# A hybrid decoder block on one core: the norm's weight in the gather's eviction, a tail in halves, and eight gate pieces inside masking and inversion

## The reference

```python
def hybrid_mixer(xn, mem_n, ...):
    p = xn @ w_in
    p_rwkv, p_swa, p_mem = jnp.split(p, [RWKV_PROJ, RWKV_PROJ + SWA_PROJ], axis=-1)
    y_rwkv = rwkv7_branch(p_rwkv, ...)      # 8 heads of 64, a recurrence over 256 tokens
    y_swa = swa_sink_alibi_branch(p_swa + b_swa, swa_sinks)
    y_mem = memory_cross_branch(p_mem, mem_n, w_mem_kv)
    branches = (y_rwkv, y_swa, y_mem)
    merged = jax.nn.sigmoid(xn @ w_gate[0]) * (branches[0] @ w_branch[0])
    for bi in range(1, N_BRANCH):
        merged = merged + jax.nn.sigmoid(xn @ w_gate[bi]) * (branches[bi] @ w_branch[bi])
    return merged @ w_out

def sparse_moe(xn, ...):                    # top 4 of 32 experts per token
    logits = (xt @ w_router + b_router)
    top_vals, top_idx = lax.top_k(logits, TOP_K)
    gates = jax.nn.softmax(top_vals, axis=-1)
    ...
        h = x_pad[tok] @ w1[e] + b1[e]      # 1024 x 2048
        return clamped_swiglu(h) @ w2[e] + b2[e]   # 1024 x 1024

h = h + hybrid_mixer(rms_norm(h, attn_norm_w), rms_norm(mem, mem_norm_w), ...)
h = h + sparse_moe(rms_norm(h, ffn_norm_w), ...)
return rms_norm(h, final_norm_w)
```

## Time and profile before

| | us |
|---|---|
| median of 3 runs | 1307.2 (1306.89 to 1308.43) |
| the profiled execution | 1308.61 |
| its span in the profile | 1306.8 |
| TensorE busy | 1222.7 (94%) |
| VectorE busy | 355.6 (27%) |
| ScalarE busy | 196.4 (15%) |

### The profile page before, as it was taken

The page is one execution under the profiler, slowest core; times in us unless marked ns, Lnnn a source line. Parts: engine busy times, 40 slices in busy tenths (PEclk is TensorE's granted clock), DMA queues, the critical chain, the costliest instruction groups (busy, mean ns, idle before and its releaser), DMA issues.

```text
span 1306.8 us, 15506 instructions
## 1 busy us (share of the span) xinstructions
PE 1222.7 (94%) x6554; PEld 597.6 (46%) x6554; DVE 355.6 (27%) x597; ACT 196.4 (15%) x377; POOL 0.2 (0%) x4
## 2 busy tenths in 40 slices
PE   8998989999999999999998989898988989898986
PEld 7886778888653333333333323232333323232322
DVE  2146472211234123221222212121222212121222
ACT  2224522200111011110101111010101111010102
POOL 0000000000000000000000000000000000000000
PEclk9999989999999999999999999999999999999999
DMA  9353201595379999999999999999999999999993
GB/s 356 106 165 129 65 4 34 191 383 200 142 268 429 427 428 429 427 428 427 428 430 427 430 427 428 429 428 430 427 427 431 427 429 428 427 431 426 429 426 164
DMA packets 51840, 449.74 MB, mean 344 GB/s; under 512 B 5552, under 2 KB 17968, under 8 KB 26704
## 3 DMA queue, kind: packets, MB, share of 16 engines
q1 hardware_dynamic: 51312, 447.49, 82.9%
q10 hardware_dynamic: 480, 1.57, 0.4%
HBM read 448.00 MB, written 1.05 MB: 344 GB/s over the span
## 4 chain that ended last, share of the span: by engine, by line
PE 63%; DMA 30%; DVE 4%; ACT 1%; issue 1%; SPq 0%; PEldq 0%; DVEq 0%
PE ps L461 62%; DMA ring<-in_w_exp 30%; DVE ring L1415 1%; PE ps L971 0%; DMA xrows<-in_x 0%; DVE upper L1506 0%; PE ps L704 0%; ACT ring L1171 0%; PE ps L613 0%; DVE ring L1412 0%; ACT ring L1197 0%; DVE upper L1463 0%; DVE merged L1441 0%; ACT upper L1140 0%; PE ps L982 0%
## 5 line engine op out<-in xcount | busy, mean ns | idle before, releaser
L461 PE MATMUL ps<-ring,upper 128*64 128x512 f32 (+4 forms) x2928 | 572.5, 535 | 38.9 <-DMA ring<-in_w_exp 35.2
L461 PEld LDWEIGHTS ps<-ring,upper 128*64 128x64 f32 (+2 forms) x2928 | 181.5, 138 | 390.4 <-issue 325.9
L461 PE MATMUL ps<-upper 128*64 128x512 f32 (+8 forms) x1644 | 288.6, 440 | 18.9 <-DMA upper<-in_w_exp 8.9
L461 PEld LDWEIGHTS ps<-upper 128*64 128x64 f32 (+4 forms) x1644 | 145.4, 161 | 154.5 <-issue 133.0
L461 PE MATMUL ps<-xT,ring 128*128 128x256 f32 x672 | 149.9, 381 | 0.4 <-DVE xT L1380 0.4
L461 PEld LDWEIGHTS ps<-xT,ring 128*128 128x128 f32 x672 | 126.5, 190 | 18.9 <-issue 1.8
L1688 DVE TENSOR_TENSOR upper<-ps,merged 128x512 f32<-128x512 f32 x32 | 22.1, 692 | 374.6 <-PEq L942 374.6
L1709 DVE TENSOR_TENSOR xrows<-xrows,ps 128x1024 f32<-128x1024 f32 x32 | 39.1, 1221 | 299.8 <-PE ps L461 299.8
L1289 ACT ACTIVATE upper<-upper 128x512 f32<-128x512 f32 x32 | 20.2, 631 | 555.5 <-DVE upper L1691 555.5
L1295 ACT ACTIVATE factors<-ps 64x512 f32<-64x512 f32 x63 | 37.3, 592 | 206.0 <-PEq L964 205.2
L461 PE MATMUL ps<-factors,upper 128*128 128x512 f32 x128 | 63.1, 617 | 0.0
(11 more groups left out here) (214 smaller groups left out, 478.2 us busy)
## 6 DMA issues: line engine op xcount, KB each, us to landing
ring<-in_w_exp SPq DMA_DIRECT2D x140, 2048.0 KB, 32.7
upper<-in_w_exp SPq DMA_DIRECT2D x48, 2048.0 KB, 33.6
ring<-in_w_gate SPq DMA_DIRECT2D x9, 1024.0 KB, 5.1
ring<-in_w_exp SPq DMA_DIRECT2D x8, 1024.0 KB, 22.0
ring<-in_w_in SPq DMA_DIRECT2D x8, 896.0 KB, 11.7
ring<-in_w_in SPq DMA_DIRECT2D x8, 640.0 KB, 3.9
ring<-in_w_branch SPq DMA_DIRECT2D x5, 1024.0 KB, 5.2
ring<-in_w_mem_kv SPq DMA_DIRECT2D x4, 1024.0 KB, 4.9
```

The costliest lines, as they stand in the source:

```text
L461: return pe.matmul(o, l, r, start=start, stop=stop, skip_group_check=True)
```

## The change

In words:

- `fill_points` gets eight new points: after the own values and transposes of the masking stage (`("gram", 0)` to `("gram", 3)`) and in levels 1 to 4 of the inversion. Each holds one piece: the four gate pieces of unit 0, then those of unit 1. The branch pieces of these units come in the first chunk's points. "rest" keeps 23 pieces. To free banks 6 and 7, the fourth `gram` group goes into banks 0 and 1 once the first is masked (`GRAM_BANK`), and `own_values` use banks 2 and 3.
- ScalarE loads the sigmoid's table ahead of the masking stage, and does the new gates between its copies.
- The norm's weight is no longer loaded as rows. `hn` is the rows times the root alone, done by ScalarE in two halves. The weight comes in as a column per partition ("ffnp", permuted on the host as the rows of `hn` are) when VectorE evicts the gather (`gathered` moves from ScalarE to VectorE).
- The transposes of the gates move into the first expert's up product, behind its fourth step. Two dummy matmuls are added in routing.
- Expert 30's second matrix is loaded as one load of 2 MB and two of 1 MB; its down product has the transposes for expert 31 and for the gates after its third quarter. The last down product uses bank 4 and `act_last`, and its four dummies are gone.
- The last scatter, addition, square, scaling and store are done by halves of 512 columns.

The diff, cut to its core:

```diff
+GRAM_BANK = (0, 2, 4, 0)
 def fill_points():
-    points = [(ch, s) for ch in range(NCH) for s in "abc"] + ["norm0", "norm1", "rest"]
-    counts = [1] * (3 * NCH) + [2, 3]
+    points = [("gram", i) for i in range(4)] + [("level", j) for j in range(1, LEVELS - 1)]
+    points += [(ch, s) for ch in range(NCH) for s in "abc"] + ["norm0", "norm1", "rest"]
+    counts = [1] * (len(points) - 3) + [2, 3]
     counts.append(PIECES * N_FILL - sum(counts))
+    sequence = [0, 1, 2, 3, 6, 7, 8, 9, 4, 5, 10, 11] + list(range(12, PIECES * N_FILL))
...
@@ SyncE
-                    load_w2(q, a, r, very_first and r == 0)
+                    if very_first and r == 0:
+                        load_w2(q, a, r, 0)
+                    elif count < GROUP and r == count - 1:
+                        load_w2(q, a, r, 2)
+                    else:
+                        load_w2(q, a, r)
...
-                    sp.wait_ge(final_sb, q * TT + t + 1)
-                    sp.dma_start(out[0, t * P:(t + 1) * P, :], outrow[:, t, :]).then_inc(stored, 16)
+                    for b in range(2):
+                        half = slice(b * 512, (b + 1) * 512)
+                        sp.wait_ge(final_sb, q * (2 * TT) + 2 * t + b + 1)
+                        sp.dma_start(out[0, t * P:(t + 1) * P, half], outrow[:, t, half]).then_inc(stored, 16)
@@ TensorE
+                if n == 3:
+                    pe.wait_ge(gram_sb, 1)
...
             pe.wait_ge(gram_sb, 2)
-            own_values(0, 0)
+            own_values(0, 2)
+            fill(("gram", 0))
+            fill(("gram", 1))
             pe.wait_ge(gram_sb, 3)
             pe.wait_ge(inv0_sb, 1)
             turn_inverse(0)
+            fill(("gram", 2))
             pe.wait_ge(gram_sb, 4)
-            own_values(1, 6)
+            pe.wait_ge(av_sb, 2)
+            own_values(1, 2)
+            fill(("gram", 3))
             pe.wait_ge(inv0_sb, 2)
             turn_inverse(1)
...
                     if j > 1:
                         turn_inverse(t)
+                if j < LEVELS - 1:
+                    fill(("level", j))
...
             gather_half(0, 1)
+            keep_awake(1, 7, const("iota"))
             pe.wait_ge(chosen_sb, 2)
...
+            keep_awake(1, 7, const("iota", 0, P))
             gather_half(1, 0)
             gather_half(1, 1)
-            pe.wait_ge(gates_sb, 1)
-            for t in range(TT):
-                last = pe.transpose(ps[0:NE, 3, t * P:(t + 1) * P], gates[:, t, :], ident)
-            last.then_inc(gT_ps, 1)
+            def turn_all_gates(c):
+                if c == 3:
+                    (the same wait and transposes)
...
-                    if final and i < 3:
-                        keep_awake(1, 4, hn[:, 0, 0:512])
+                    if between:
+                        between(i)
                 pe.wait_ge(slots_used, n + (NMIX + 1))
                 pe.sem_inc(down_ps, 1)
-                if final:
-                    keep_awake(1, 4, hn[:, 0, 0:512])
...
-            up(g, r, E, N, 0, None, first)
+            up(g, r, E, N, 0, turn_all_gates if very_first else None, first)
...
+                def turns(i):
+                    if i == 2:
+                        turn(E + 1)
+                        turn_gates(N, False)
+                if last:
+                    down(q, g, r, E, 2, False, turns)
@@ ScalarE
+            act.activation(ss[:, 7:8], epsc[:, 0:1], ACT.Sigmoid)
-            act.dma_start(ffnw, ffn_norm_w.to_broadcast([P, D])).then_inc(late_loaded, 16)
...
+                act.wait_ge(norm_scale, t + 1)
+                for b in range(2):
+                    half = slice(b * 512, (b + 1) * 512)
+                    act.activation(hn[:, t, half].rearrange("p (c q) -> p q c", c=4), xrows[:, t, half].rearrange("p (q c) -> p q c", c=4),
+                                   ACT.Copy, scale=ss[:, 4 + t:5 + t]).then_inc(hn_sb, 1)
...
-                    act.activation(outrow[:, t, :], xrows[:, t, :], ACT.Square, accum_out=ss[:, t:t + 1]).then_inc(fin_ss, 1)
+                    act.activation(outrow[:, t, 0:512], xrows[:, t, 0:512], ACT.Square, accum_out=ss[:, t:t + 1]).then_inc(norm_ss, 1)
+                    act.activation(ss[:, 2 + t:3 + t], ss[:, t:t + 1], ACT.Identity, scale=1.0 / D, bias=epsc[:, 0:1]).then_inc(norm_ss, 1)
+                    act.activation(outrow[:, t, 512:D], xrows[:, t, 512:D], ACT.Square, accum_out=ss[:, t:t + 1]).then_inc(norm_ss, 1)
+                    act.activation(ss[:, 4 + t:5 + t], ss[:, t:t + 1], ACT.Sqrt, scale=1.0 / D, bias=ss[:, 2 + t:3 + t]).then_inc(norm_rt, 1)
@@ VectorE
-                normed_half(0)
-                normed_half(1)
+            def gathered(N, very_first=False):
+                for b in range(2):
+                    if b == 0 or very_first:
+                        dve.wait_ge(xg_ps, N + 1 + (b if very_first else 1))
+                    TTn(xg[:, 4 * b:4 * b + 4, :], ps[:, 4 + b, :].rearrange("p (c s) -> p c s", c=4),
+                        prm[:, PCOLS["ffnp"] + 4 * b:PCOLS["ffnp"] + 4 * b + 4].unsqueeze(2).to_broadcast([P, 4, P]), ALU.mult).then_inc(xg_sb, 1)
...
                 swiglu(E + 1)
+                if not last:
+                    gathered(N + 1)
...
-                add_up(N, 0)
-                add_up(N, 1, False, 0)
+                add_halves(q, N, 0, 6)
+                add_halves(q, N, 1, 0)
```

More of the change, by code:

```diff
@@ L705, in turn_inverse, with piece, fill @@
                 last.then_inc(turned_ps, 1)
+            def piece(p):
+                m, r = p // PIECES, p % PIECES
+                b, f = UNITS[m]
+                if r < 4:
+                    if r == 0 and m:
+                        pe.wait_ge(gate_sb, m)
+                    w = take("gate", (b, f))
+                    for k in (2 * r, 2 * r + 1):
+                        for ff in range(2):
+                            last = mm(half(6, ff), w[:, k * 256 + ff * P:k * 256 + (ff + 1) * P], xT[:, k, :],
+                                      k == 0 and ff == 0, k == KC - 1)
+                            if k == 0 and ff == 0 and (m == 1 or m and m % 2 == 0):
+                                last.then_inc(slots_used, 1)
+                    if r == 3:
+                        last.then_inc(gate_ps, 1)
+                else:
+                    if r == 4 and m:
+                        pe.wait_ge(merged_sb, m)
+                    w = take("branch", (b, f // 2))
+                    for k in (2 * (r - 4), 2 * (r - 4) + 1):
+                        for ff in range(2):
+                            at = k * 512 + (f % 2) * 256 + ff * P
+                            last = mm(half(7, ff), w[:, at:at + P], (gT, y_swa, y_mem)[b][:, k, :], k == 0 and ff == 0, k == 3)
+                            if k == 0 and ff == 0 and m != 1:
+                                last.then_inc(slots_used, 1)
+                    if r == 5:
+                        last.then_inc(branch_ps, 1)
+            points = fill_points()
+            def fill(point):
+                for p in points[point]:
+                    piece(p)
             pe.wait_ge(gram_sb, 2)
-            own_values(0, 0)
+            own_values(0, 2)
+            fill(("gram", 0))
+            fill(("gram", 1))
             pe.wait_ge(gram_sb, 3)
@@ L942, in up, with down @@
                 pe.sem_inc(up_ps, 1)
-            def down(q, g, r, E, final=False, very_first=False):
+            def down(q, g, r, E, whole=4, final=False, between=None):
                 pe.wait_ge(actT_sb, E + 1)
+                bank, hidden = (4, act_last) if final else (3, actT)
                 for i in range(4):
@@ L993, in scatter @@
                     last = mm(ps[:, bank + n, :], selgT[:, t, :], yrow[:, n * 512:(n + 1) * 512])
+                    if halves and n == 0:
+                        last.then_inc(sc_half, 1)
                 last.then_inc(sc_ps, 1)
@@ L1219, in gates_of @@
                         gate(p // PIECES)
+            act.activation(ss[:, 7:8], epsc[:, 0:1], ACT.Sigmoid)
+            own_values(0, 2)
+            turned_inverse(0, 0)
+            own_values(1, 2)
+            gates_of(("gram", 3))
+            turned_inverse(0, 1)
+            for j in range(1, LEVELS - 1):
+                for t in range(TT):
+                    turned_inverse(j, t)
+                gates_of(("level", j))
             def by_heads(a):
@@ L1708, in add_up, with add_halves @@
                 a = xrows[:, t, :].rearrange("p (b n) -> p b n", b=2)
-                TTn(a, a, ps[:, bank:bank + 2, :], ALU.add).then_inc(acc_sb, 1)
+                TTn(a, a, ps[:, 6:8, :], ALU.add).then_inc(acc_sb, 1)
+            def add_halves(q, N, t, bank):
+                for b in range(2):
+                    half = slice(b * 512, (b + 1) * 512)
+                    if b == 0:
+                        dve.wait_ge(sc_half, q * TT + t + 1)
+                        dve.wait_ge(acc_sb, N * 2 + t)
+                    else:
+                        dve.wait_ge(sc_ps, N * 2 + t + 1)
```

(1 more changed line is left out.)

170 lines of the change are left out of this document (67 added, 103 removed).

## The result

The changed kernel took 1298.96 us (median of 4 runs, 1296.22 to 1299.65) where the kernel before took 1307.05 (4 runs, 1305.95 to 1308.43): a ratio of 0.9934, 95% interval 0.9921 to 0.9947. That is 8.1 us faster, inside the range, and 2.6 us above the forecast of 1296.4. Run again beside nine runs of the kernel before, it took 1297.75 against 1307.09, ratio 0.9929 (0.9915 to 0.9942), 9.3 us. The profiled execution took 1299.14 us, with a span of 1297.0; that of before took 1308.61.

What follows compares the result with a forecast made beforehand. Weight loads were taken to pace the expert stage, so gains lie only before the first slot's return and behind the last weights: 3.6 + 2.0 + 5.2 = 10.8 us, giving a median of 1296.4 us, range 1292.7 to 1302.7.

Steps and rivals of the forecast that it cites:

- The front's term: Masking to chunks: moving eight gate pieces out of "rest" frees 13.8 us, costs 4.2, 5.6 and 0.4 elsewhere, gains 3.6 us.
- Masking: Masking stage up to level 1's second product: five gate pieces fill TensorE's waits at full clock, costing only 4.2 us.
- The list of blocks: TensorE's sequence in masking from 166.72 us: own values, pieces, transposes, products and 0.4 for tile-shape changes, 14.1 us together.
- Inversion: Inversion levels 2 to 4: no hole, so three pieces cost 1.73 us each plus some 0.15 for the switch, 5.6 us.
- Merge: Start of the chunks: piece 10 waits until VectorE has merged unit 0, costing 0.4 us.
- Routing: Gather to first expert: 0.5 us from moving the gates' transposes, 1.5 from dummies keeping the clock up, together 2.0 us.
- the sentence that the waits which the dummies fill are the only ones: Routing: two dummy matmuls fill TensorE's only two waits there, so 1.5 us was taken for a gather at full clock.
- Down products: Last two experts' down products: 0.9 us earlier up to the last one, which then runs without dummies; 4.4 us gained.
- the sentence that the weights are no limit: Last down product: DMA engines are done by 1286 us and the last quarter starts at 1287.5, so no load delays it.
- Scatter to end: Last scatter, norm and stores by halves: earlier computing, and 0.6 us from a half-size last store; together 0.8 us.

## Why the prediction came out

It was right on the sign and inside its range; its sum had one term too small, one too large, and one right for a false reason. The front's term came out 1.4 us above the forecast and the last stretch 0.5 below, so the total is in part luck. Point by point, with the table's stretches:

**Masking, forecast 4.2 us for five pieces, measured 3.5.** The list of blocks was right. What did not come are the 0.4 us for changes of tile shape; the rest is that a block's duration overlaps the start of the next by about 0.1 us, and I had added durations where starts were wanted. Against the second profile of before, whose clock fell later, it is 3.7. TensorE runs through and the clock is 1.00 from 168 to 176, as forecast.

**Inversion, forecast 5.6, measured 4.9.** From level 1's second product to the chunks there are 21.14 us instead of 16.20 (176.57 to 192.77): 4.94 for three pieces. That there is no hole in a level was right: a level with a piece takes 5.66 us, its old 3.93 and the piece's 1.73. What failed is the 0.15 per piece for the switch, which didn't come, and the last level, which I left as it was and which is 0.25 us shorter. I had also read gaps of 0.15 us between all six blocks of a level; the trace has one such gap in each, ahead of the second xx product, and a wait of 0.41 us in the last level, at 192.77.

**Merge, forecast 0.4, measured 0.3.** The front's gain up to routing is then 13.8 - 3.5 - 4.9 - 0.3 = 5.1, read from the last norm's transposes as 5.0, against 3.6 forecast (the transposes begin at 348.99 instead of 353.44, and the own values 0.52 later). The term was mis-sized by small allowances, each on the same side.

**Routing, forecast 2.0, measured 1.85** (6.82 of front less 4.97, or 26.23 - 24.38). The amount is right: 1.5 for the gather, 0.5 for the transposes, less small change. The cause is wrong, and the 1.5 us were right by luck. The step that failed is the sentence that the waits which the dummies fill are the only ones and so decide the clock. There is a third, of 0.19 us ahead of the router's product, in both kernels. Without dummies the clock stays as well, and with the old routing it falls in both profiles.

**Down products, forecast 4.4, measured 4.5** (from the start of expert 30's down product to ScalarE's copy: 1293.80 - 1273.16 = 20.64 us before, 1283.76 - 1267.66 = 16.10 after). The split is a little different: 1.4 us instead of 0.9 up to the last down product, 3.1 instead of 3.5 in it. There the sentence that the weights are no limit failed by 0.3 us: the front's gain did not change the order, but a down product without dummies closes up to its last load and waits for it.

**Scatter to end, forecast 0.8, measured about 0.3.** The computing gave 0.1 to 0.2 as forecast, the smaller last store 0.2 instead of 0.6. The rule of the Trainium skill (DMA: Bandwidth & Descriptors, Anatomy of one DMA), a fixed time plus bytes over bandwidth, is fitted there to DMAs that GpSimd issues, and these stores are SyncE's. By its figures they would land after an estimated 2.6 and 3.2 us; over all stores the trace comes near that (2.7 and 3.3 us in the mean of the profiles' medians). The step that failed was to give the missing bytes' 0.6 us to the last of four stores issued within 2.85 us: it takes 3.1 us in the mean, where a last store of 512 KB takes 3.3.

**What no term had.** Around the span there are some 2.12 us instead of 1.79 in every run of the changed kernel: 0.3 us lost. The kernel with tripled evictions is back at 1.77, and it stores just as the changed one does, while the one with two whole stores has 2.11, so it isn't the number of stores; what it is stays open.

**The sum.** For the profiled execution, stretch by stretch: -0.5 (start) + 6.8 + 3.9 - 0.4 - 0.3 = 9.5 us, its 1308.61 - 1299.14. For the second profile of the changed kernel: 0.2 + 6.8 + 4.4 + 0.4 - 0.3 = 11.5. The forecast of 10.8 lies between them. The medians differ by 8.1 and 9.3 only. Both profiled executions of the kernel before (1308.61 and 1308.86) lie 1.4 to 1.8 us above its median, so a sum against them, carried over to the median unchanged, most likely took as gain a part that the median doesn't have. Which stretch of before is shorter in its other executions can't be seen, since those have no profile.

## What to carry to other kernels

Work that fits anywhere is best put where TensorE waits for another engine, even for tenths of a microsecond at a time: eight pieces of 13.8 us cost 8.7 there, and the clock, which had fallen to half in the masking, stayed at 1.00. Most of that gain is in the masking, where the waits were 0.9 to 1.6 us; in the levels three pieces of 5.2 us cost 4.9. A stretch that a stream of loads paces can swallow what is added to an engine that isn't the bottleneck (2.75 us of VectorE work in each of 15 pairs, no effect), so look for gains only ahead of the moment that releases the stream and behind its last byte. And when a gain comes out as forecast, take its supposed cause out by itself: here the two dummies were in the sum at 1.5 us, the 1.5 us came, and the dummies had nothing to do with it.

## What the runs showed of the hardware that I had not expected

- With very nearly the same matmuls and waits (0.43 and 0.30 us, 0.51 and 0.23 us), TensorE's clock falls to half at the gather in the kernel before, in both its profiles, and stays at 1.00 in the three kernels with the new routing and no dummies, one profile each. The cause is open.
- Where the clock falls isn't fixed even within one kernel. In the masking it fell to 0.81 of full in the window of 168 to 170 us in one profile of before; in the other it was still 1.00 from 170 to 172, with TensorE busy 0.48 of the 2 us:

```profile
170.00:172.00 2.00, 0.48 (x15) 0.45 (x16) 1.90 (x4) 0.60 (x1) 0.00 (x0) 1.00 0.00 0
172.00:174.00 2.00, 1.97 (x29) 1.71 (x24) 1.13 (x2) 0.74 (x2) 0.00 (x0) 0.50 0.00 0
```

  The clock fell when the matmuls had come back, and ran at half speed through work that had no wait. The Trainium skill (TensorE: Matmul & The Clock Gate, Part 1) says that the monitor's intervals run freely and don't begin with the kernel, which would let the fall move like this; no run here tests it.
- 2.9 us of spread between executions lie ahead of the first masking product: in the two compared, 1.3 us in how soon the first projections begin, behind the first input rows, and 1.6 in the projections themselves.
- Four stores of 256 KB in a row end only 0.2 us sooner than two of 512 KB, although the median store lands 0.6 us sooner after its issue: the last of the four takes 3.1 us in the mean, the first 2.5.
